# A mixture-of-experts weight ring of eight slots instead of six, with buffers that share storage to make room for it

## What is computed

```python
def moe_swiglu(h, router, w13, w2):
    '''Top-2-of-8 routing, softmax over the selected logits; experts evaluated densely, sparse combine.'''
    logits = (h @ router).astype(F32)
    top_val, top_idx = lax.top_k(logits, TOP_K)
    weights = jax.nn.softmax(top_val, axis=-1)
    ...
```

## Time and profile before

| What | us |
|---|---|
| Median of 3 runs | 2292.82 (2289.87 to 2294.31) |
| The profiled execution's own time | 2290.82 |
| Its span | 2288.6 |
| PE busy | 2127.0 (93%) |
| DVE busy | 1154.9 (50%) |
| ACT busy | 921.0 (40%) |
| First expert load issued by SP | at 1318.0 |
| First expert product on PE | at 1357.9 |
| Last expert product on PE | ends at 2273.5 |

### The profile page before, as it was taken

The page is one execution under the profiler, slowest core; times in us unless marked ns, Lnnn a source line. Parts: engine busy times, 40 slices in busy tenths (PEclk is TensorE's granted clock), DMA queues, the critical chain, the costliest instruction groups (busy, mean ns, idle before and its releaser), DMA issues.

```text
span 2288.6 us, 55584 instructions
## 1 busy us (share of the span) xinstructions
PE 2127.0 (93%) x24430; PEld 1569.9 (69%) x24430; DVE 1154.9 (50%) x1544; ACT 921.0 (40%) x1208; POOL 197.2 (9%) x200
## 2 busy tenths in 40 slices
PE   8999999999999999999999889987998799879977
PEld 4677667788888658888888769834983498349822
DVE  2544795422232486666666358702870387028702
ACT  4422023422222375555555257503750375037500
POOL 2000471100000022000000130000000000000000
PEclk9999999999999999999999999999999999999999
DMA  8566307233222511212121279999999999999997
GB/s 286 188 226 231 111 3 237 77 101 98 92 92 92 172 57 61 62 57 62 62 62 28 87 286 379 351 407 405 405 357 407 405 405 358 407 405 404 359 390 280
DMA packets 229009, 512.10 MB, mean 224 GB/s; under 512 B 15367, under 2 KB 108447, under 8 KB 228511
## 3 DMA queue, kind: packets, MB, share of 16 engines
q1 hardware_dynamic: 225950, 498.18, 59.2%
q10 hardware_dynamic: 1730, 7.10, 0.9%
q0 software_dynamic: 1152, 4.19, 0.6%
HBM read 492.67 MB, written 16.78 MB: 223 GB/s over the span
## 4 chain that ended last, share of the span: by engine, by line
PE 74%; DMA 10%; SPq 6%; DVE 4%; ACT 3%; issue 2%; POOL 0%; ACTq 0%; DVEq 0%
PE bank L1785 14%; DMA expert_w<-in_moe_w_dram 7%; PE bank L1815 7%; SPq L924 6%; PE bank L1868 4%; PE bank L1257 4%; PE bank L1258 4%; PE bank L1259 4%; PE bank L1134 2%; PE bank L1389 2%; PE bank L1163 2%; PE bank L1135 2%; PE bank L1136 2%; DMA arena<-in_rw_w_rkv_dram 2%; PE bank L1275 2%
## 5 line engine op out<-in xcount | busy, mean ns | idle before, releaser
L3289 DVE TENSOR_TENSOR w_low<-expert_w,w_high 128x1792 fp32r<-128x1792 f32 (+1 forms) x192 | 386.0, 2024 | 123.4 <-ACT w_high L2420 121.9
L2420 ACT CAST w_high<-expert_w 128x1792 fp32r<-128x1792 f32 (+1 forms) x192 | 325.1, 1700 | 112.6 <-PE bank L1785 80.6
L1868 PE MATMUL bank<-expert_w,arena 128*64 128x448 f32 x1024 | 204.6, 550 | 36.0 <-DMA expert_w<-in_moe_w_dram 26.2
L1868 PEld LDWEIGHTS bank<-expert_w,arena 128*64 128x64 f32 x1024 | 76.8, 139 | 156.0 <-issue 155.4
L1785 PE MATMUL bank<-w_high,xg_high 128*128 128x448 f32 x512 | 150.7, 376 | 30.7 <-DVE xg_low L3279 30.7
L1785 PE MATMUL bank<-w_low,xg_high 128*128 128x448 f32 x512 | 149.5, 374 | 0.0
L1785 PE MATMUL bank<-w_high,xg_low 128*128 128x448 f32 x512 | 149.0, 373 | 0.0
L3386 DVE TENSOR_TENSOR arena<-arena,bank 128x448 f32<-128x448 f32 x16 | 9.9, 621 | 263.1 <-PE bank L1868 263.1
L1257 PE MATMUL bank<-u_high,ring_high 128*128 128x512 f32 x352 | 139.7, 397 | 1.8 <-DVE u_low L2935 1.8
L1258 PE MATMUL bank<-u_low,ring_high 128*128 128x512 f32 x352 | 139.5, 396 | 0.0
L1259 PE MATMUL bank<-u_high,ring_low 128*128 128x512 f32 x352 | 138.8, 394 | 0.0
(11 more groups left out here) (474 smaller groups left out, 4128.4 us busy)
## 6 DMA issues: line engine op xcount, KB each, us to landing
expert_w<-in_moe_w_dram SPq DMA_DIRECT2D x128, 1792.0 KB, 13.4
expert_w<-in_moe_w_dram SPq DMA_DIRECT2D x32, 2048.0 KB, 16.7
arena<-in_mod_w_dram SPq DMA_DIRECT2D x48, 1024.0 KB, 8.4
expert_w<-in_moe_w_dram SPq DMA_DIRECT2D x32, 1536.0 KB, 16.8
arena<-in_ffn_w_dram SPq DMA_DIRECT2D x44, 512.0 KB, 5.2
arena<-in_hy_w_in_dram SPq DMA_DIRECT2D x12, 1024.0 KB, 5.3
arena<-in_rw_w_rkv_dram SPq DMA_DIRECT2D x48, 256.0 KB, 3.0
arena<-in_ffn_w_dram SPq DMA_DIRECT2D x11, 1024.0 KB, 4.9
```

Of the source, the lines that this page charges most:

```text
L1868: last = pe.matmul(b[hd(v), 0:EH], small_x[:, k, :], w[:, kk, v * EH:v * EH + EH], start=(k == 0), stop=(k == KT - 1))
L2420: act.copy(high_piece(kind, n), piece(kind, ering[q % ERN], n // 2, n % 2))\
L3289: dve.tensor_tensor(piece(kind, low[s], n // 2, n % 2), piece(kind, ering[s], n // 2, n % 2), high_piece(kind, n).bitcast(F32), ALU.subtract)\
```

## The change

- `ERN` goes from 6 to 8. Load q goes to slot q modulo 8 and waits for the product of load q - 8. The rows are fetched and stored ahead of load 10 of an item instead of load 8 (`ERN + 2`).
- The slots 6 and 7 lie over the squares of the LayerNorm and the first tiles of the output projection's weights, so the first loads into them wait for `ln_scaled` at 24. The slots count on the semaphores `w_loaded` of the older ring; 6 and 7 get new ones.
- `rt_w` and the order table move to a place that the RWKV pairs leave free. SP loads them before the output projection's weights, ahead of `pair_done`.
- To make room, `OUT` shares storage with `high[2]`, `rowg` and `rowb` with `high[3]`, and `expert_rows` with `UTOK[:, 0]`. `XGH`, `small_x`, `pickT`, `moved` and `small_hid` move too.
- Hence `rowg` and `rowb` are loaded by SP after the last expert load, and no longer by ACT during the LayerNorm; and ACT's `yield_small` first waits until `rows_moved` is 64.

```diff
-ERN = 6
+ERN = 8
...
-        OUT = sb(2, D)
...
-        expert_rows = arena[:, mark() + D:mark() + 2 * D]
...
+        early_slots = [s for s in range(ERN) if slot_at[s] + slot_words[s] <= sq_at]
...
+        OUT = arena[:, high_at[2]:high_at[2] + 2 * D].rearrange("p (t d) -> p t d", d=D)
+        rowg, rowb = (arena[:, high_at[3] + D * i:high_at[3] + D * i + D] for i in range(2))
...
+        expert_rows, gathered_rows = UTOK[:, 0, :], UTOK[:, 1, :]
...
+        ring_loads = ffn_start + FT + FT // 2 + 5
+
+        def expert_landed(s):
+
+            return sem(f"w_loaded{s}"), 16 * ((ring_loads - s + RN - 1) // RN) if s < RN else 0
...
+            load("ld_tail", rt_w, a["moe_router"][0].rearrange("(k p) e -> p k e", p=P))
+            load("ld_tail", order_table, consts[4])
             for k in range(KT):
                 load("ld_out", WO[k], a["rw_w_out"][k * P:(k + 1) * P, :])
                 sp.wait_ge(sem("ld_out"), 16 * (k + 1))
             sp.wait_ge(sem("pair_done"), 2)
 
-            load("ld_tail", rt_w, a["moe_router"][0].rearrange("(k p) e -> p k e", p=P))
-            load("ld_tail", order_table, consts[4])
...
-            def load_large(couple, item, e):
+            def load_large(couple, item, e, first=False):
                 for q, (kind, c, half) in enumerate(LOADS):
-                    if q == 8:
+                    if q == ERN + 2:
                         fetch_rows("small_gathered", couple - 1, item)
...
+                    if first and q < ERN and q not in early_slots:
+                        sp.wait_ge(sem("ln_scaled"), 24)
                     load_expert(kind, c, half, q % ERN, e)
...
+            for name, row in (("ln_g", rowg), ("ln_b", rowb)):
+                load("ld_last_rows", row, a[name][1, 1:2, :].partition_broadcast(P))
             for tt in range(2):
                 sp.wait_ge(sem("final"), tt + 1)
...
-            for name, row in (("ln_g", rowg), ("ln_b", rowb)):
-                load("ld_last_rows", row, a[name][1, 1:2, :].partition_broadcast(P))
             ln_root(3, SEQ)
...
             def yield_small(couple):
                 step(act, "expert_products", f"small_down{EC - 1}_1", couple - 1)
+                act.wait_ge(sem("rows_moved"), 64)
                 act.wait_ge(sem("rows_out"), 48 * couple + 16)
```

More of the change, by code:

```diff
@@ L512, in build @@
         BON, Gf = sb(SEQ), sb(SEQ)
+        pair_table_end = mark()
         assert mark() <= table + 3400
@@ L577, in build @@
         XTOK = sb(2, D)
-        rt_w, logit, mx, ixf, comb = sb(KT, N_EXP), sb(2, 8), sb(2, 8), sb(2, 8), sb(2, 8)
+        logit, mx, ixf, comb = sb(2, 8), sb(2, 8), sb(2, 8), sb(2, 8)
         ix = sb(16).bitcast(U32)
@@ L585, in build @@
         second, row_of, row_parts = sb(2, 8), sb(2, 8), sb(4, 8)
-        order_table = sb(6 * N_EXP + P)
-        tie, rank_of, capacity, capacity_1, jump, row_base = (order_table[:, N_EXP * j:N_EXP * j + N_EXP] for j in range(6))
-        small_no = order_table[:, 6 * N_EXP:]
         facts, ranked = sb(6, N_EXP), sb(6, N_EXP)
@@ L591, in build @@
         place, hot, counts = ranked[:, 0:2, :], ranked[:, 2:4, :], ranked[:, 4, :]
+        mark(max(mark(), pair_table_end))
+        rt_w, order_table = sb(KT, N_EXP), sb(6 * N_EXP + P)
+        tie, rank_of, capacity, capacity_1, jump, row_base = (order_table[:, N_EXP * j:N_EXP * j + N_EXP] for j in range(6))
+        small_no = order_table[:, 6 * N_EXP:]
+        pickT = sb(2, P)
         key, rank, over = sb(N_EXP), sb(N_EXP), sb(N_EXP)
@@ L604, in build @@
         mark((mark() + 7) // 8 * 8)
-        XGL = split("xg_low", mark(), KT, P)
-        mark(mark() + KT * P)
+        XGL, XGH = split("xg_low", mark(), KT, P), split("xg_high", mark() + KT * P, KT, P)
+        small_x = arena[:, mark():mark() + KT * SMALL].rearrange("p (k t) -> p k t", t=SMALL)
+        mark(mark() + 2 * KT * P)
         assert mark() <= table
@@ L613, in build @@
         mark(mark() + sum(slot_words))
-        OUT = sb(2, D)
-        mark((mark() + 7) // 8 * 8)
-        XGH = split("xg_high", mark(), KT, P)
-        mark(mark() + KT * P)
+        early_slots = [s for s in range(ERN) if slot_at[s] + slot_words[s] <= sq_at]
         HTH = split("hid_high", mark(), EF, P)
         HTL = split("hid_low", mark() + EW, EF, P)
+        moved = arena[:, mark():mark() + 6 * N_EXP * N_EXP].rearrange("p (n j e) -> p n j e", j=N_EXP, e=N_EXP)
+        small_hid = arena[:, mark() + EW:mark() + EW + EF * SMALL].rearrange("p (f t) -> p f t", t=SMALL)
         mark(mark() + 2 * EW)
-        small_x = arena[:, mark():mark() + KT * SMALL].rearrange("p (k t) -> p k t", t=SMALL)
-        small_hid = arena[:, mark() + D // 2:mark() + D // 2 + EF * SMALL].rearrange("p (f t) -> p f t", t=SMALL)
-        moved = arena[:, mark() + D:mark() + D + 6 * N_EXP * N_EXP].rearrange("p (n j e) -> p n j e", j=N_EXP, e=N_EXP)
-        expert_rows = arena[:, mark() + D:mark() + 2 * D]
[L625 to L628, removed]
+        high_at = [ut_at + PIECE * i if i < 2 else mark() + PIECE * (i - 2) for i in range(PIECES)]
+        high = [split(f"w_high{i}", high_at[i], 1, PIECE)[:, 0, :] for i in range(PIECES)]
+        OUT = arena[:, high_at[2]:high_at[2] + 2 * D].rearrange("p (t d) -> p t d", d=D)
+        rowg, rowb = (arena[:, high_at[3] + D * i:high_at[3] + D * i + D] for i in range(2))
         mark(mark() + 2 * PIECE)
@@ L631, in build @@
         slot_share = sb(8)
-        rowG, rowg, rowb = sb(D), sb(D), sb(D)
+        rowG = sb(D)
         UTOK = sb(2, D)
-        gathered_rows = UTOK[:, 1, :]
+        expert_rows, gathered_rows = UTOK[:, 0, :], UTOK[:, 1, :]
         assert mark() <= ARENA, (mark(), ARENA)
@@ L836, in _ @@
                 sp.dma_start(ring[s].rearrange("p (k n) -> p k n", n=D), gap_weights(1, i)).then_inc(w_loaded[s], 16)
+            assert ld.n == ring_loads
             sp.wait_ge(sem("out_full"), 2 * KT)
@@ L923, in load_expert @@
                     dst = ering[s][:, 0:KT * EH].rearrange("p (k n) -> p k n", n=EW)
-                sp.dma_start(dst, src).then_inc(sem(f"ew_loaded{s}"), 16)
-            def load_large(couple, item, e):
+                sp.dma_start(dst, src).then_inc(expert_landed(s)[0], 16)
+            def load_large(couple, item, e, first=False):
                 for q, (kind, c, half) in enumerate(LOADS):
-                    if q == 8:
+                    if q == ERN + 2:
                         fetch_rows("small_gathered", couple - 1, item)
@@ L954, in _ @@
             with sp.Fori(0, n_passes) as p:
-                load_large(p * PAIRS, p * N_EXP, 0)
+                load_large(p * PAIRS, p * N_EXP, 0, first=True)
                 sp.wait_ge(sem("routed"), 3)
@@ L1854, in landed @@
                 q = LOADS.index((kind, c, half))
-                pe.wait_ge(sem(f"ew_loaded{q % ERN}"), 16 * len(LOADS) // ERN * (2 * couple + 1) + 16 * (q // ERN + 1))
+                weights, before_ = expert_landed(q % ERN)
+                pe.wait_ge(weights, 16 * len(LOADS) // ERN * (2 * couple + 1) + before_ + 16 * (q // ERN + 1))
                 settle(pe)
@@ L2416, in high_digits @@
                     if n % 2 == 0:
-                        act.wait_ge(sem(f"ew_loaded{q % ERN}"), 16 * len(LOADS) // ERN * 2 * item + 16 * (q // ERN + 1))
+                        weights, before_ = expert_landed(q % ERN)
+                        act.wait_ge(weights, 16 * len(LOADS) // ERN * 2 * item + before_ + 16 * (q // ERN + 1))
                     kind0, c0, half0 = LOADS[q - PIECES // 2]
```

## The result

| | before | after |
|---|---|---|
| Median, us | 2291.36 (4 runs, 2289.87 to 2294.31) | 2267.23 (4 runs, 2265.56 to 2269.67) |
| The profiled execution | 2290.82 | 2267.49 |
| Its span | 2288.6 | 2265.4 |

The ratio is 0.9896 [0.9881, 0.9912], 24 us faster. (A ratio is that of the record, with its 95% interval in brackets; it can differ from the quotient of the two medians by some 0.0005.) Run again later beside the other experiments, the changed kernel had a ratio of 0.9913 [0.9897, 0.9929] (2268.78 against 2287.46), 19 us. Forecast were 22.5 us.

The account below looks back on a forecast made before the run. The prediction took the experts to be bound by the flow of weights, lost only where it is not full. Terms -9.0 - 20.7 + 2 + 5.2 = -22.5 us took the median 2292.8 to 2270.3, range 2262 to 2281.

Parts of the forecast that it names:

- The bound: In the experts: the flow of weights sets the time, and only time in which the flow is not full is lost.
- Two more loads ahead at the start: First large item: loads 6 and 7 are fetched early and stay in hand at its end, 9.0 us faster.
- the head start is not gained: Rival, 4%: loads 6 and 7 come too late or ACT's wait costs PE as much; 9.0 us less gain, 2279.3.
- The three later large items: Late in each, the flow loses 6.9, 6.7 and 7.1 us; eight slots regain 20.7 us, less 2 given back.
- The tables: Router weights and order table loaded before the output projection's weights: 0 us, 1 us if SP's waiting did not cover it.
- ACT's wait: First large item, ACT waiting for the scatters: ACT 1 to 2 us late, PE with 3 us in hand, 0 us.
- The rows at the end: The last LayerNorm's rows land 2.6 us behind the last weights and uncover 5.5 us of DVE work: +5.2 us.
- The slower rival: Rival, 3%: with up to seven loads queued the full flow itself drops; at 3% it costs 27 us, giving 2297.

Follow-up runs that it names:

- experiments 1 and 2: The changed kernel with six slots, 2295.96 us (ratio 1.0033 to the kernel before), and with one of its eight slots left unused, 2276.93 us (ratio 0.9951).
- Experiment 3: The changed kernel with loads 6 and 7 of the first item issued no sooner than with six slots: 2269.31 us, ratio 0.9912 to the kernel before.
- experiment 4: The changed kernel with ACT's wait for the four scatters moved to the head of the first large item: 2281.43 us, ratio 0.9975 to the kernel before.
- experiment 6: The kernel before with only router weights and order table loaded ahead of the output projection's weights: 2287.13 us against 2287.46, ratio 0.9999.
- experiment 5: The kernel before with only the last LayerNorm's two rows loaded by SP behind the last expert load: 2294.54 us against 2287.46, ratio 1.0027.
- experiment 9: The changed kernel with DVE's wait for the last rows moved to their first use: 2265.48 us, run again 2262.60, ratio 0.9891 to the kernel before both times.

## Why the prediction was right, and where it was not

**The bound.** Flow of weights, lost only where the slots were full: right. It is shown by experiments 1 and 2, in which the flow late in the large items goes with the number of slots while all else stays.

**Two more loads ahead at the start, 9.0 us.** The size was right (9.9 and 11.3 us in couple 1), the reason half wrong. The step said both that the two loads are fetched in the rest before 1365 and that the item then ends "with two more loads in hand". Only the second matters. Experiment 3 took the first away at no cost. So the rival "the head start is not gained", priced at 9.0 us, had no price at all as far as the loads go: the first large item has flow to spare. Its other half, a wait of ACT that costs PE its start, would have been paid in full, as experiment 4 shows, but the change's own wait did not hold up PE (see below).

**The three later large items, 20.7 us less 2.** The flow recovered as forecast: 406, 399 and 403 GB/s leave 0, 1.0 and 0.5 us of the three losses, 1.5 where I took 2. Less of it reached the end. Couples 2 and 3 together took 457.9 us before and 446.8 and 448.3 after: 11.0 and 9.5 us, where the forecast has 6.9 + 6.7 - 1.4 = 12.2. Couple 4, read without the rows' wait, brings 248.1 - 242.3 = 5.8 and 5.0, where it has 7.1 - 0.7 = 6.4. The sum, 14.5 to 16.8, is 2 to 4 us under the 18.7. I took a couple at 222 us of flow; couple 2 took 224 to 225.6 at a full 405 GB/s, moving about 1 MB more than couple 3 between the same marks. The bytes account for what is missing in couples 2 and 3: between the marks the changed kernel moved 180.8 and 181.5 MB in its two profiles, the kernel before 180.2, and the 0.5 and 1.3 MB more are 1.3 and 3.1 us at 406 GB/s, where 1.2 and 2.7 are missing. A mark at a landing may cut the flow at another byte when five loads are under way; that was not tested. It suits this that couples 1 to 3 together are as forecast: they bring 20.9 and 20.8 us, and the forecast has 9.0 + 12.2 = 21.2. The split between the couples was off more than their sum.

**The tables.** 0 us, shown in experiment 6.

**ACT's wait.** ACT stood still for 3.0 us, where I had 1 to 2 us of lateness:

```profile
1359.49 0.69 ACT L2437 ACTIVATE arena<-bank,arena 128x512 f32<-128x512 f32 x1 [3.04 <-DMA slot_rows<-arena]
1360.08 4.87 ACT L2430 CAST w_high<-expert_w 128x1792 fp32r<-128x1792 f32 x3
```

PE was not held up: the first large item, from its first product to the small item's first, took 123.7 us (1354.12 to 1477.77) against 124.1 before. The cover, the four gate pieces, held.

**The rows at the end, +5.2 us.** Shown in its size and in each step: rows 2.4 to 2.6 us behind the last weights, 5.3 us from the product to L3414. By experiment 5 it is 5.5 us in the last column, by experiment 9 4 to 7. Not foreseen was 0.6 us more in the first profile, where PE's matmuls after its wait ran at the lower clock; in the second profile the same four took 1.13 us, and nothing was added. What I did not draw from this step is that nothing between the wait and L3425 reads the rows; the price was for the place of a wait, and the step had all that was needed to see it.

**The sum.** Forecast -22.5 us, 2270.3; measured 2267.23. The 24 us of the first comparison hold, in the profiled execution, some 4 us of chance ahead of the experts, and by that luck it lies on the far side of the forecast. The experts' part alone gave 19.4 and 21.8 us in the two profiles, and the second comparison 19. For the first profile, the terms are -9.9 (couple 1), -11.0 (couples 2 and 3), -5.8 (couple 4 without the wait) and +7.4 (249.7 against 242.3, the wait), in sum -19.3. Against -22.5 the forecast was 3 us too good, 2 in the later couples and 2 at the end, less 1 in couple 1.

**The slower rival.** A full flow that suffers from up to seven loads under way can't be seen here, since so many never were: see the last section.

## What to carry to other kernels

A ring between a steady flow and stages that use it at different rates needs room for the surplus of the fast-fed stage, here 129.6 - 111 = 19 us of flow, and each slot up to that pays by degrees; how early the ring is filled does not matter while the first stage has flow to spare. When buffers are merged, look for the load that has to move behind its old cover, and then put its wait at the first instruction that reads it, not at the head of the block (4 to 7 us here by the profiles). Mark stages by an event on the critical chain and subtract: that told 5 us at the end from 4 us of chance some 900 us earlier.

## What the runs showed of the hardware that was not expected

SP's own issue instruction blocks when enough is under way. The lengths of its issues of expert loads from 1560 to 1800 (min/median/max in ns), in the kernel before:

```profile
L924 SPq DMA_DIRECT2D expert_w<-in_moe_w_dram x51: 372/388/6103, 1559.5 to 1796.7; - x51
```

and in the changed kernel:

```profile
L930 SPq DMA_DIRECT2D expert_w<-in_moe_w_dram x52: 368/3918/6445, 1560.1 to 1797.0; - x52
```

The median went from 0.39 to 3.9 us, but it mixes two kinds of stretch. By stretches, with the median time to landing of the same loads:

| Stretch | before: issue, landing (us) | after: issue, landing (us) |
|---|---|---|
| 1600 to 1640, in the large item | 0.37, 13.1 | 3.9, 21.2 |
| 1660 to 1710, late in the large item | 0.37, 9.2 | 0.37, 15.0 |
| 1720 to 1800, in the small item | 4.1, 21.8 | 4.1, 21.9 |

So SP is held with six slots too, wherever landing is near 21 us; eight slots only add the first part of the large item to this. Landing stayed near 21 us in the small items, where I forecast near 30, also with more free slots. At 4.52 us a load, about five loads of 1792 KB seem to be all that this queue takes before the issue itself blocks; what the limit counts was not tried. No run shows a cost of it here, as the flow was full, but anything SP issues next waits as well: in the changed kernel its load of `ln_g` lasted 3.14 us at 2224.1.
